# Gathering the U and V rows of a PEER layer with one indirect DMA per slot, or with two

## What is computed

```python
q = (xc @ wq).reshape(PEER_CHUNK, PEER_HEADS, PEER_DK)
s1 = einsum('thd,hnd->thn', q[..., :D_HALF], keys[0]); s2 = einsum(..., q[..., D_HALF:], keys[1])
v1, i1 = top_k(s1, 16); v2, i2 = top_k(s2, 16)
cand = v1[..., :, None] + v2[..., None, :]          # 256 pairs of a head
best, pos = top_k(cand, 16); idx = cand_idx at pos  # 16 experts of 16384
g = softmax(best)
act = gelu(einsum('td,thkd->thk', xc, u_tab[idx]))
return einsum('thk,thkd->td', g * act, v_tab[idx])
```

## Time and profile before

| | before |
|---|---|
| median of three runs | 3542.14 us |
| profiled execution, its span (first to last instruction) | 3538.8 us |
| mean granted TensorE clock | 0.847 |
| busy: PE, DVE, ACT, POOL | 69%, 75%, 20%, 39% |
| DMA engines' mean busy share, by queue: gathers (q0), SP's (q1) | 77.5%, 13.1% |
| moved | 1213.87 MB, 343 GB/s |

### The profile page before, as it was taken

One profiled execution on the slowest core, in us unless ns is written; L12 is line 12 of the kernel. 1 busy time (PEld: TensorE's weight loads), 2 busy tenths in 40 slices (PEclk: granted clock), 3 DMA queues, 4 the chain that ended last, 5 costly groups with the idle time before them and its releaser, 6 DMA issues.

```text
span 3538.8 us, 29116 instructions
## 1 busy us (share of the span) xinstructions
PE 2458.2 (69%) x7568; PEld 1327.5 (38%) x7568; DVE 2665.5 (75%) x6520; ACT 690.5 (20%) x1951; POOL 1370.9 (39%) x1296
## 2 busy tenths in 40 slices
PE   8459986579999695676878787667576555554554
PEld 7437453246545352223544343334222212211221
DVE  1575779866778699896768788779867587777776
ACT  2021311121444111112114333111111111111111
POOL 0032322333344333443434445435444444444443
PEclk9779998889999898887988889888888867767767
DMA  7889698889888998899999899999888899999997
GB/s 214 267 287 343 255 357 311 298 324 359 334 321 337 340 363 312 328 338 353 400 398 366 352 361 383 379 354 381 347 346 350 332 382 385 377 367 371 373 381 294
DMA packets 330478, 1213.87 MB, mean 343 GB/s; under 512 B 20705, under 2 KB 186593, under 8 KB 198881
## 3 DMA queue, kind: packets, MB, share of 16 engines
q0 software_dynamic: 147456, 1073.81, 77.5%
q1 hardware_dynamic: 182880, 138.45, 13.1%
HBM read 1198.54 MB, written 13.63 MB: 343 GB/s over the span
## 4 chain that ended last, share of the span: by engine, by line
PE 34%; DVE 29%; DMA 23%; ACT 5%; issue 5%; SPq 2%; POOL 2%; POOLq 0%; DVEq 0%; ACTq 0%
DMA ring<-in_uv,cur_idx 19%; PE vacc L926 16%; DVE ring L1107 11%; PE bank L964 6%; DVE acc L1138 4%; ACT diag L751 3%; PE bank L1032 3%; PE o_ps L930 2%; POOL ring L714 2%; PE bank L960 1%; DMA wpool<-in_w_in 1%; PE bank L1043 1%; DVE lt L1255 1%; DVE ocT L1265 1%; PE bank L975 1%
## 5 line engine op out<-in xcount | busy, mean ns | idle before, releaser
L926 PE MATMUL vacc<-ring,diag 128*128 128x512 f32 x2048 | 1260.7, 759 | 988.9 <-ACT diag L751 988.6
L714 POOL DMA_INDIRECT ring<-in_uv,cur_idx x1024 | 1205.7, 1177 | 1206.9 <-PE vacc L926 667.9
L1107 DVE CUSTOM_DVE_ANT_0 ring<-ring,xn 128x1024 f32<-128x1024 f32 x1024 | 1220.6, 1222 | 364.8 <-DMA ring<-in_uv,cur_idx 338.4
L926 PEld LDWEIGHTS vacc<-ring,diag 128*128 128x128 f32 x2048 | 480.0, 245 | 1668.2 <-ACT diag L751 1031.3
L1138 DVE SCALAR_TENSOR_TENSOR acc<-ring,g_w,acc 128x512 f32<-128x512 f32 x832 | 625.6, 752 | 35.2 <-DVE g_w L1130 0.6
L705 POOL COPY cur_idx<-idx 128x4 uint32<-128x4 uint32 (+1 forms) x256 | 163.1, 637 | 931.4 <-DVE acc L1138 713.5
L746 ACT ACTIVATE g_ex<-g_cu 128x4 f32<-128x4 f32 x256 | 52.5, 205 | 2077.8 <-DVE g_cu L1120 2077.8
L751 ACT ACTIVATE diag<-ident,g_w 128x128 f32<-128x128 f32 x1024 | 326.8, 390 | 186.0 <-DVE g_w L1130 185.7
L964 PE MATMUL bank<-hT,wpool 128*128 128x256 f32 (+2 forms) x1280 | 288.0, 385 | 10.7 <-DMA wpool<-in_w_in 9.3
L964 PEld LDWEIGHTS bank<-hT,wpool 128*128 128x128 f32 x1280 | 221.9, 194 | 79.1 <-issue 21.7
L1043 PE MATMUL bank<-hT,wpool 128*128 128x256 f32 (+2 forms) x1024 | 239.0, 390 | 5.2 <-DMA wpool<-in_peer_wq 4.5
(11 more groups left out here) (129 smaller groups left out, 1809.2 us busy)
## 6 DMA issues: line engine op xcount, KB each, us to landing
wpool<-in_w_in SPq DMA_DIRECT2D x96, 512.0 KB, 8.3
wpool<-in_peer_wq SPq DMA_DIRECT2D x64, 512.0 KB, 8.5
wpool<-in_w_out SPq DMA_DIRECT2D x32, 512.0 KB, 6.7
ring<-in_uv,cur_idx POOLq DMA_INDIRECT x1024, 8.9
xb<-in_x SPq DMA_DIRECT2D x15, 512.0 KB, 8.6
x_scratch<-xb SPq DMA_DIRECT2D x8, 512.0 KB, 6.7
xn_scratch<-xb SPq DMA_DIRECT2D x8, 512.0 KB, 7.1
xn<-xn_scratch SPq DMA_DIRECT2D x8, 512.0 KB, 7.5
```

The source lines that it names most:

```text
L714: nc.gpsimd.indirect_dma_start(ring[:, s, :], None, uv, bass.IndirectOffsetOnAxis(ap=cur_idx[:, s:s + 1], axis=0))\
L926: ins = nc.tensor.matmul(vacc[:, :], diag[:, q, s, :], ring[:, q * GROUP + s, D:D + PE_COLS], start=first and s == 0, stop=last and s == G ...
L1107: ins = nc.vector.tensor_tensor_reduce(out=ring[:, s, 0:D], in0=ring[:, s, 0:D], in1=xn[:, c % 2, :], scale=1.0, scalar=0.0, op0=ALU.mult, ...
```

## The change

The two tables stay apart. Each slot is fetched by two indirect DMAs of 128 rows of 4 KB, one into `u_ring` and one into `v_ring`, which each have 8 slots of 1024 floats. The two rings together take the bytes of the old one. On POOL a group is now: wait that the dots of group G - 2 are done (`s_dot`) and that the V gathers of G - 2 have landed (as their indices are about to be written over); copy the indices; issue the four U gathers; then for each of the four slots wait for `s_vd` and `s_vp` as before and issue the V gather. VectorE's dots wait for `s_gatu`, its additions and TensorE's matmuls for `s_gatv`. Two waits that the old order implied are written out: ScalarE's diagonals wait for `s_vp`, and VectorE's weights for `s_diag`, both of group G - 2.

```diff
-        ring = sb("ring", [P, RING, 2 * D])
+        u_ring = sb("u_ring", [P, RING, D])
+        v_ring = sb("v_ring", [P, RING, D])
...
-                used = (n * 2 + q - 2) * GROUP
+                G = n * 2 + q
+                used = (G - 2) * GROUP
                 very_first = c == 0 and isinstance(i, int) and i == 0
                 if not very_first:
-                    pool.wait_ge(s_vd, used + 1)
+                    pool.wait_ge(s_dot, G - 1)
+                    for s in range(q * GROUP, (q + 1) * GROUP):
+                        pool.wait_ge(s_gatv[s], n * 16)
                 sl = slice(q * GROUP, (q + 1) * GROUP)
                 nc.gpsimd.tensor_copy(cur_idx[:, sl], idx[:, c % KEEP, bass.ds(i * RING + q * GROUP, GROUP)])\
                     .then_inc(s_idx, 1)
-                pool.wait_ge(s_idx, n * 2 + q + 1)
+                pool.wait_ge(s_idx, G + 1)
                 pool.sem_inc(s_go, 1)
+                for s in range(q * GROUP, (q + 1) * GROUP):
+                    nc.gpsimd.indirect_dma_start(u_ring[:, s, :], None, u_tab,
+                                                 bass.IndirectOffsetOnAxis(ap=cur_idx[:, s:s + 1], axis=0))\
+                        .then_inc(s_gatu[s], 16)
                 for s in range(q * GROUP, (q + 1) * GROUP):
                     if not very_first:
                         pool.wait_ge(s_vd, used + s % GROUP + 1)
                         pool.wait_ge(s_vp, used + s % GROUP + 1)
                         pool.sem_inc(s_go, 1)
-                    nc.gpsimd.indirect_dma_start(ring[:, s, :], None, uv,
+                    nc.gpsimd.indirect_dma_start(v_ring[:, s, :], None, v_tab,
                                                  bass.IndirectOffsetOnAxis(ap=cur_idx[:, s:s + 1], axis=0))\
-                        .then_inc(s_gat[s], 16)
+                        .then_inc(s_gatv[s], 16)
...
                 act.wait_ge(s_gw, n * 2 + q + 1)
+                if not (c == 0 and isinstance(i, int) and i == 0):
+                    act.wait_ge(s_vp, (n * 2 + q - 1) * GROUP)
...
                 for s in range(GROUP):
-                    ins = nc.tensor.matmul(vacc[:, :], diag[:, q, s, :], ring[:, q * GROUP + s, D:D + PE_COLS],
+                    pe.wait_ge(s_gatv[q * GROUP + s], (n + 1) * 16)
+                    ins = nc.tensor.matmul(vacc[:, :], diag[:, q, s, :], v_ring[:, q * GROUP + s, 0:PE_COLS],
...
                 if part == 2:
+                    if not (c == 0 and isinstance(i, int) and i == 0):
+                        dve.wait_ge(s_diag, G - 1)
                     weights(G, sl)
...
-                    dve.wait_ge(s_gat[s], (n + 1) * 16)
-                    ins = nc.vector.tensor_tensor_reduce(out=ring[:, s, 0:D], in0=ring[:, s, 0:D],
+                    dve.wait_ge(s_gatu[s], (n + 1) * 16)
+                    ins = nc.vector.tensor_tensor_reduce(out=u_ring[:, s, :], in0=u_ring[:, s, :],
...
                     s = q * GROUP + k
-                    nc.vector.scalar_tensor_tensor(out=acc[:, c % 2, PE_COLS:D], in0=ring[:, s, D + PE_COLS:2 * D],
+                    dve.wait_ge(s_gatv[s], (G // 2 + 1) * 16)
+                    nc.vector.scalar_tensor_tensor(out=acc[:, c % 2, PE_COLS:D], in0=v_ring[:, s, PE_COLS:D],
...
-    data["uv"] = _np.concatenate([data["peer_u"][0], data["peer_v"][0]], axis=1)
+    data["peer_u"], data["peer_v"] = data["peer_u"][0], data["peer_v"][0]
```

More of the change, by code:

```diff
@@ L311, in bank_frees, with build @@
     return []
-def build(nc, x, w_in, w_out, wq, keys, uv, cols_in, g_ffn, g_fin, out):
+def build(nc, x, w_in, w_out, wq, keys, u_tab, v_tab, cols_in, g_ffn, g_fin, out):
     line = timeline()
@@ L412, in build @@
         xbflat = xb[:, :, :].rearrange("p a d -> p (a d)")
-        key_src = ring[:, 0, :].rearrange("p (t n) -> p t n", t=LISTS)
+        key_src = u_ring[:, 0:2, :].rearrange("p s d -> p (s d)").rearrange("p (t n) -> p t n", t=LISTS)
         keys_home = vN[:, CHUNKS // 2:, :].rearrange("p c n -> p (c n)")
@@ L496, in build @@
         s_go = sem("s_go")
-        s_gat = [sem(f"s_gat{i}") for i in range(RING)]
+        s_gatu = [sem(f"s_gatu{i}") for i in range(RING)]
+        s_gatv = [sem(f"s_gatv{i}") for i in range(RING)]
         s_dot = sem("s_dot")
@@ L929, in group @@
                     if wide:
-                        ins = nc.tensor.matmul(o_ps[:, :], diag[:, q, s, :], ring[:, q * GROUP + s, D + PE_COLS:2 * D],
+                        ins = nc.tensor.matmul(o_ps[:, :], diag[:, q, s, :], v_ring[:, q * GROUP + s, PE_COLS:D],
                                                start=first_wide and s == 0, stop=last and s == GROUP - 1,
@@ L1373, in _ @@
                             group(c, i, q, part, False, False)
-_ARGS = ["x", "w_in", "w_out", "peer_wq", "peer_keys", "uv", "cols", "ffn_norm_g", "final_norm_g"]
+_ARGS = ["x", "w_in", "w_out", "peer_wq", "peer_keys", "peer_u", "peer_v", "cols", "ffn_norm_g", "final_norm_g"]
 def kernel(**inputs):
```

## The result

The changed kernel takes 3673.26 us (median; 3657.83 to 3683.55). Measured beside it, the kernel before takes 3542.16 us; the ratio is 1.0366, with a 95% interval of 1.0336 to 1.0396. The forecast was 3705 us in a range of 3585 to 3810 us. The profiled execution has a span of 3681.5 us, 142.7 us more than that of before.

The account below looks back on a forecast made before the run. The DMA engines were taken to bound the kernel from 1600 us on, then POOL's issue: 159.6 groups at 13.0 us for 11.96 add 166 us, earlier stages 0, so 3538.8 + 166 = 3705 us; range 3585 to 3810 us.

Parts of the forecast that it names:

- The bound of before: From 1600 us on the DMA engines are the wall, at shares of 0.89 to 0.99, with groups of 11.3 to 12.7 us.
- The bound moves to POOL's issue: Wherever a group now takes less than 13 us, POOL's eight issues set the pace, above the DMA engines' 11.1 us.
- The price of a group: POOL waiting for nobody: issues 9.42, gaps 2.10, rest 1.48, together 13.0 us; lower end 10.8, upper end 16.0 us.
- The sum: From 1600 us on, 159.6 groups go from 11.96 to 13.0 us, + 166 us; before 1600 us, 0.
- The DMA engines: Gather packets of 4 KB at 0.173 us, 11.1 us a group; share in 2800 to 3400 us falls to about 0.85.
- The landing: Sign of a right forecast: landing of gathers falls to 4 to 5 us, from 8.9 us.
- What costs nothing: New waits before the copy, for V in VectorE and PE, and for group G - 2 cost nothing, covered by 12 us.
- Faster, as a half-size gather costs half: Rival: issue costs by bytes, POOL needs 8.3 us a group; 3430 to 3500 us; chance 0.10 with the other faster case.
- Faster, as POOL's issues don't hold back the queue: Rival: DMA engines stay the wall with no gaps; 3430 to 3500 us; chance 0.10 with the other faster case.
- No change: Rival: POOL at about 12 us a group, loss in chunks 6 and 7 paid back earlier; 3540 us; chance 0.04.
- A loss by dear packets: Rival: 4 KB packets need 11.9 us a group from 1600 us; 3650 us with cheap POOL, 3740 with it; chance 0.06.

## Why the prediction was right, step by step

**The bound of before.** It was put on the DMA engines from 1600 us on. The pair of kernels with half V rows shows it: a quarter less bytes takes 189 us from the kernel before. Of these some 24 us come ahead of 1600 us (511 POOL instructions up to there, 501 before, so two groups), the rest behind it.

**The bound moves to POOL's issue.** Shown from four sides: small extra gathers do the same harm and more, taking bytes away hardly helps, shorter issues help by just their sum, and six issues a group do little.

**The price of a group.** Forecast 13.0 us, measured 12.8 us from 1600 us on and 12.9 us in 2800 to 3400 us. The parts, from the groups of POOL's instructions in that last stretch:

```profile
L723 POOL DMA_INDIRECT v_ring<-in_peer_v,cur_idx x185 | 236.3, 1277 | 56.4 <-issue 56.4
L715 POOL DMA_INDIRECT u_ring<-in_peer_u,cur_idx x188 | 207.0, 1101 | 82.6 <-issue 35.1 <-POOL cur_idx L710 33.2 <-DVE acc L1153 11.6
L710 POOL COPY cur_idx<-idx 128x4 uint32 (+1 forms) x46 | 17.9, 389 | 0.2
```

The eight issues take 4 x 1.277 + 4 x 1.101 = 9.51 us (forecast 9.42); that V issues are the longer ones is as told, the dots fall beside them. The seven gaps of 0.30 us hold but for a few longer ones (up to 1.9 us), which make up the 0.1 us between the sum below and 12.9 us. The copy takes 0.39 us, not 0.64; the 0.34 us ahead of it are gone, as no V addition is waited for; the 0.5 us from copy to first issue are 0.81 us, for which the wait that was taken out had wrongly been given credit. 9.51 + 2.10 + 0.39 + 0.81 = 12.8 us. So the close agreement is in part luck: two errors of 0.3 us cancelled, and the third is the 0.25 us of the copy.

**The sum.** Forecast + 166 us from 1600 us on, measured span + 142.7 us. It splits so: 159.6 groups x (12.82 - 11.96) = 137 us; 1.3 groups more are still to be done at 1600 us (256 - 160.9 = 95.1 were behind it; before it was 96.4), 17 us, where the forecast had put 0; and the end behind the last issue is 18.8 us where it was 30.0 us, - 11 us. That is U ahead: the last diagonals start 12.6 us behind the last issue (3508.8 us) in the kernel before and 1.6 us behind it (3662.7 us) in the changed one, as the last dots no longer follow it. First the kernel before, then the changed one:

```profile
3521.48 1.28 ACT L751 ACTIVATE diag<-ident,g_w 128x128 f32<-128x128 f32 x4 [0.72 <-DVE g_w L1130]
```

```profile
3664.23 1.28 ACT L762 ACTIVATE diag<-ident,g_w 128x128 f32<-128x128 f32 x4 [0.80 <-DVE g_w L1144]
```

The term that was too large is the group, by 0.2 us or 29 us in all; the two terms that had been put at 0, + 17 and - 11 us, nearly cancel. The medians are 131 us apart, as this profiled execution (3683.55 us) lies 10 us above its median.

**The DMA engines.** This step failed in size, and without harm: the share in 2800 to 3400 us was to fall to about 0.85 and is 0.92. A 4 KB packet with its share of small ones was put at 0.173 us. It was 0.801 x 3681.5 x 16 / 262144 = 0.180 us, 7% over half of the old 0.335. But not the row's length alone does that. With the extra gathers of 64-byte rows, the kernel with the old 8 KB rows has

```profile
q0 software_dynamic: 180224, 1082.26, 77.9%
```

which is 0.779 x 3760.8 x 16 / 131072 = 0.358 us for an 8 KB packet with its small ones; the extra gathers' own packets are in this time. The kernel with half as many of them bounds their part: its queue (78.6% of 3562.8 us) took 925 us of engine time more than before's, and with the extra gathers behind every slot it is 2994 us more. Twice 925 us can be the packets themselves, some 4%; the other 1100 us, some 3%, come only with POOL at eight issues a group (why, no run here shows). 4 KB rows against 8 KB rows in kernels with eight issues are 0.180 against half of 0.358, which is the same within 1%, or within 3% if the extra gathers' data packets are taken out. So the row's length is the lesser part of the 7% at most.

A DMA share of 0.92 was no sign of a wall: with a quarter of the bytes gone the share in chunks 6 and 7 was still 0.78, and a group was only 0.3 us shorter. The landing was forecast at 4 to 5 us and is longer. In the group of the timeline above, the first U gather is issued at 3108.96 us and the dot that waits for it starts 5.6 us later; for the next two it is 6.3 and 6.5 us:

```profile
3114.54 1.23 DVE L1121 CUSTOM_DVE_ANT_0 u_ring<-u_ring,xn 128x1024 f32<-128x1024 f32 x1 [1.51 <-DMA u_ring<-in_peer_u,cur_idx]
```

**What costs nothing.** The new waits in VectorE's additions for V (95.7 us over the span, 2.1 us at the longest) and in PE's matmuls are visible and don't set the pace in the late stages, where POOL does not wait for V's users. This was as told. No run tried them where POOL isn't the bound.

**The rivals.** "Faster, as a half-size gather costs half" fell with the issues of 64-byte rows at 1.135 us. "Faster, as POOL's issues don't hold back the queue" fell with the extra gathers (6.6% slower); in the changed kernel four more issues a group cost 3.7%. The Trainium skill's page "DMA: Bandwidth & Descriptors" (anatomy of one DMA) calls descriptor generation small, with many descriptors before its cost shows; at 1.12 to 1.21 us of POOL for an indirect DMA of 128 rows the measurement differs, and decides. "No change" needed 1.05 us an issue; that price appears only with halved dots. A loss by dear packets is bounded by the 36 us that half V rows give back, and in chunks 6 and 7 even that is shorter issues.

## What to carry to other kernels

Count what a change adds to the engine that issues the transfers, and compare it with the period of the stage, not with that engine's share of the span: 39% busy left room for two more issues in a group of 11.4 us and not for four. An indirect DMA costs its issuer by the instruction (128 rows each in all runs here) and not by the bytes, so fetching the same bytes in rows of half the length doubles the issuer's work for nothing. Starting a transfer earlier does not pay for that: U ahead is worth 1.2% where the split alone costs 5.2%, and it gave nothing in the late stages, where POOL itself had no time left.

## What the runs showed of the hardware

The issue of an indirect DMA of 128 rows takes POOL about the same for rows of 64 bytes, 4 KB and 8 KB: 1.135, 1.118 to 1.211 and 1.177 us in the mean, and 0.30 us pass between two of them. Issues of 4 KB rows are lengthened where a dot of VectorE, an operation of two inputs, runs beside them: halved dots bring the mean from 1.15 to 1.05 us. With POOL as the bound, the busy share of the DMA engines fell less than the rate: a quarter less bytes in the gathers took it from 0.92 to 0.78, at 256 GB/s in place of 330. The recorded time of the gather queue for an 8 KB packet with all small ones grew from 0.335 to 0.358 us when POOL issued twice as many DMAs, and by the kernel with six issues at most some 4% of this 7% are the added packets themselves.
